# Layer 0's first eight units on the unscaled input, its first two half by half, and the input's hi halves one pair later

## The chip, the cores and the metric

The kernel runs on one core of a Trainium2 chip. The metric is device time in microseconds, from one launch to its end; three runs of the kernel before gave a median of 1510.79 us. "hi" and "lo" below are the two parts into which every fp32 operand is split, so that a product can be made of three fp32r matmuls (hi·hi, lo·hi, hi·lo).

## What is computed

One step of a two-layer decoder on 320 tokens (256 of a prompt, 8 x 8 of samples), width 1024, weights in fp32. Each layer, cut to what matters here:

```python
h = rms_norm(x, g_mix_pre)
proj = h @ w_in                      # split into q, k, v, g_ret, ca, cb, ga, gb
u = ca * sigmoid(cb)                 # conv branch: 16 units of weights, done first
z = conv(concat([c0, u]), conv_w)    # 31 taps per channel, depthwise
y_ret = (silu(g_ret) * layer_norm(retention(q, k, v, r0))) @ w_ret_out
x = x + rms_norm((sigmoid(ga)*y_ret + sigmoid(gb)*(silu(ln(z)) @ w_conv_out)) @ w_o, g_mix_post)
h2 = rms_norm(x, g_ffn_pre)
x = x + rms_norm((silu(h2 @ w_ffn_gate) * (h2 @ w_ffn_up)) @ w_ffn_down, g_ffn_post)
```

`rms_norm(x, g)` is x times g per channel times one factor per token. The factor (`rstd`) can be applied to x before the product with the weights, or to the product afterwards.

## The kernel before

All tensors lie with channels on partitions: x is 8 tiles of 128 channels by 320 tokens. The weights come as 360 units of 128 x 8 x 128 (512 KB), 180 per layer, in the order in which they are used, through a ring of four buffers. For each unit SyncE loads `wring`, ScalarE copies the hi part into `whi`, VectorE subtracts it and writes `wlo` (the helper `lower`), and TensorE runs 24 matmuls into one of four banks (`unit`). `split(l, u)` on ScalarE and on VectorE stands for unit u + 3 (AHEAD): it is made three units ahead, into the buffer that unit u - 1 gave back. Semaphores carry the order; within an engine the order is that of the code.

Units 0 to 15 of a layer are its input to the conv branch, in pairs: unit 2n gives cb, unit 2n + 1 gives ca of tile n. VectorE makes u of tile n (`up` for the prompt, `us` for the samples). Then come four heads of 12 units (`head`), and the rest.

Layer 0: ScalarE squares x, VectorE adds the squares, TensorE takes their mean, ScalarE makes `rstd`, and VectorE makes h (`normalised`): the value in `acc`, its hi part on ScalarE (`hhi`), its lo part (`hlo`). Only then does TensorE begin: `first_units` runs units 0 to 2 side by side, tile of h by tile of h; unit 3 and three rounds of four units (`cin_round`) follow, all on h.

Layer 1: units 0 to 7 (pairs n < FREE_PAIRS = 4) run on x times g only (`uhi`, `ulo`), while the statistics are taken in between; VectorE multiplies each product by `rstd` when it reads the bank (into `sig`, then `tmp`; both count `cin_step`). h for the rest is made along with these pairs, H_TILES = (0,1,2), (3,4,5), (6,7) tiles behind pairs 0, 1 and 2, and TensorE waits for all eight (`h_ready`) before unit 8:

```python
if free and n < len(H_TILES):
    for k in H_TILES[n]:
        h_value_of(l, k)
    if n:
        for k in H_TILES[n - 1]:
            h_low_of(l, k)
```

GpSimd works in layer 0 in this order: it starts the transfers (params, conv state, constants, two retention states), waits until all eight tiles of h are there (`h_ready`), computes the 30 old taps of the samples' convolution (`past_taps`, 60 tensor operations), stores the conv results (`cp_out`, `cs_out`), waits until these are stored, and then serves the heads: as soon as VectorE has updated a quad of retention states it stores the quad (`rs_out`) and loads the next but one (`state`) into the same buffer. TensorE reads that one in the next head's units (`late_query`, at unit 4, tile 3 and unit 5, tile 3).

Of the kernel before, what the change touches and what calls it, by code (L numbers as in the profile page):

```python
# [113 lines left out]
def program(nc, w, xin, consts, params, r_in, c_in, x_out, rp_out, rs_out, cp_out, cs_out):  # L114
    ctx = ExitStack()
    with ctx:
# [30 lines left out]
        gpre = sb("gpre", KT)  # L147
# [27 lines left out]
        past0 = sb("past0", KT, DB, DS, offset=go_at + (HEADS - 1) * 4 * T * 4 + KT * DB * DS * 4)  # L175
# [61 lines left out]
        gpre_loaded = sem("gpre_loaded")  # L237
# [23 lines left out]
        x_loaded, par_loaded, con_loaded = sem("x_loaded"), sem("par_loaded"), sem("con_loaded")  # L261
# [42 lines left out]
        def _(pool):  # L304
# [91 lines left out]

            pool.dma_start(par[:, :], params[0]).then_inc(par_loaded, 16)
# [4 lines left out]
            pool.dma_start(gpre[:, :], params[1, :, G_MIXPRE:G_MIXPRE + KT]).then_inc(gpre_loaded, 16)  # L402
            for l in range(DEPTH):
                for q in range(2):
                    load(l, q)
                if l == 0:
# [4 lines left out]
                    past_taps(0, past0, stap, par[:, G_CB:G_CW], par[:, G_CW:NPAR])  # L411
# [36 lines left out]
            pool.wait_ge(gpre_loaded, 16)  # L448
# [5 lines left out]
        def _(pe):  # L454
# [25 lines left out]
            def first_units(l, q, rhs, hi_ready, ready, between=None):  # L480

                pe.wait_ge(lo_done, l * UNITS + (q * RING + AHEAD))
                for k in range(UB):
# [10 lines left out]
                    if between is not None:  # L494
                        between(k)

# [218 lines left out]
            for l in range(DEPTH):  # L715

                if l == 0:
                    keep_clock(18)
                    for k in (0, 1, 4, 5):
                        pe.wait_ge(x_halves, k // 4 + 1)  # L720
                        mm = pe.matmul(X[:, 0:T], ones_d[:, :], sq8[:, k, :], start=(k == 0), stop=(k == 5))
                    mm.then_inc(stat_done, 1)
                    keep_clock(12)

                def x_half(i):

                    pe.wait_ge(x_halves, l * 2 + (i + 1))
                    if i == 0:
# [12 lines left out]
                def cin_round(i, rhs):  # L741
                    for j in range(4):
                        if j % 2 == 0:
# [5 lines left out]
                if l == 0:  # L749
                    first_units(l, 0, h_tile, lambda k: pe.wait_ge(h_hi, l * 16 + (k + 1)), lambda k: h_read(l, k))  # L750
                    unit(l, 0, AHEAD, AHEAD, h_tile)
                    with pe.Fori(1, 4) as i:
                        cin_round(i, h_tile)
                else:
                    first_units(l, 0, u_tile, lambda k: pe.wait_ge(ux_hi, (l - 1) * KT + (k + 1)), lambda k: pe.wait_ge(ux_ready, (l - 1) * KT + (k + 1)), between=x_both)
                    unit(l, 0, AHEAD, AHEAD, u_tile)
                    cin_round(1, u_tile)
                    pe.wait_ge(h_ready, l * 16 + KT)
                    with pe.Fori(2, 4) as i:
                        cin_round(i, h_tile)  # L760
# [108 lines left out]
        def _(act):  # L869
# [142 lines left out]
            log_exp_table()  # L1012
            act.wait_ge(x_loaded, 16)
            for k in range(KT):
                act.activation(sq8[:, k, :], x[:, k, :], ACT.Square).then_inc(sq_done, 1)
            act.wait_ge(memset_done, 2)
# [14 lines left out]
            for s in range(AHEAD - 1):  # L1031
                first_split(s)
            for l in range(DEPTH):
                if l:
                    split(l, U_CIN)
                act.wait_ge(stat_done, l * STATS + 1)
                rsqrt(l, X[:, 0:T], 0, 0)
                if l == 0:
                    first_split(AHEAD - 1)
                if l == 0:  # L1040
                    halves_of_h(l, range(KT))
# [686 lines left out]
```

## Time and profile before

| | |
|---|---|
| median of three runs | 1510.79 us (1508.86 to 1515.58) |
| time of the profiled execution | 1509.68 us |
| its span from first to last instruction | 1507.9 us, so 1.8 us lie around it |
| TensorE busy, share of the span | 97% |
| mean granted TensorE clock | 0.996 of 2.4 GHz |
| TensorE's first unit begins | 15.10 us |
| unit 8 of layer 0 begins | 43.37 us |
| unit 8 of layer 1 begins | 793.38 us |

The profile is of one execution. Each timeline row gives start, duration, engine, line and operation, and in brackets how long the engine sat idle before it and whose signal ended that. A matmul of a unit starts every 0.147 us at full clock, so a unit takes 3.52 us.

### The profile page before, as it was taken

The numbers are of one execution on the slowest core, as the hardware profiler recorded it, in microseconds if no ns is written. First come the engines' busy times: TensorE is split into PE (matmuls) and PEld (weight loads), VectorE is DVE, ScalarE is ACT, GpSimd is POOL, SyncE is SP. The second block draws the span as 40 slices with busy tenths as digits, with TensorE's granted clock in tenths as the row PEclk, the third lists the DMA queues.
The fourth block names the chain that finished last, engine by engine and source line by source line (L and its number), as shares of the span: only waits on it lengthen the run. The fifth ranks groups of instructions, "written<-read, shape, count | busy, mean of one in ns | idle before, by whom it ended". The sixth has DMA issues, their size and how long they took to land.

```text
span 1507.9 us, 25284 instructions
## 1 busy us (share of the span) xinstructions
PE 1466.7 (97%) x9684; PEld 1374.0 (91%) x9684; DVE 1138.6 (76%) x1771; ACT 678.8 (45%) x996; POOL 276.9 (18%) x254
## 2 busy tenths in 40 slices
PE   9999999999999999999989999999999999999997
PEld 8997978888999899999979979788799999999996
DVE  6999999989666677885478897989885766666544
ACT  5343534446454443443353445345554645434432
POOL 4991212120300002555100001122111000000000
PEclk9999999999999999999999999999999999999999
DMA  8447665855545254445535565757654442544453
GB/s 330 144 154 263 235 243 197 316 196 193 162 133 190 84 171 150 153 141 168 168 129 168 187 222 215 276 199 293 219 182 145 142 152 85 168 153 151 154 155 122
DMA packets 64970, 275.46 MB, mean 183 GB/s; under 512 B 7280, under 2 KB 7536, under 8 KB 55664
## 3 DMA queue, kind: packets, MB, share of 16 engines
q1 hardware_dynamic: 53280, 193.49, 39.2%
q0 software_dynamic: 11600, 80.74, 14.1%
q8 instruction: 61, 1.00, 0.3%
q14 instruction: 29, 0.24, 0.0%
HBM read 230.30 MB, written 43.89 MB: 182 GB/s over the span
## 4 chain that ended last, share of the span: by engine, by line
PE 78%; DVE 12%; DMA 4%; ACT 3%; issue 2%; POOL 0%; DVEq 0%; ACTq 0%; POOLq 0%
PE bank L466 23%; PE bank L468 22%; PE bank L467 22%; DVE wlo L1164 3%; DMA state<-r_in 3%; DVE acc L1207 2%; DVE state L1238 2%; DMA rs_out<-state 1%; PE bank L628 1%; PE bank L609 1%; PE bank L645 1%; PE bank L491 1%; DVE x L1560 1%; ACT whi L878 1%; PE bank L577 1%
## 5 line engine op out<-in xcount | busy, mean ns | idle before, releaser
L466 PE MATMUL bank<-hhi,whi 128*128 128x320 f32 x1976 | 638.3, 323 | 7.3 <-DVE hlo L1164 5.3
L1164 DVE TENSOR_TENSOR wlo<-wring,whi 128x1024 fp32r<-128x1024 f32 x363 | 483.8, 1336 | 186.7 <-ACT whi L878 159.7
L468 PE MATMUL bank<-hhi,wlo 128*128 128x320 f32 x1976 | 612.2, 310 | 0.0
L467 PE MATMUL bank<-hlo,whi 128*128 128x320 f32 x1976 | 612.0, 310 | 0.0
L466 PEld LDWEIGHTS bank<-hhi,whi 128*128 128x128 f32 x1976 | 372.3, 188 | 28.7 <-issue 27.6
L467 PEld LDWEIGHTS bank<-hlo,whi 128*128 128x128 f32 x1976 | 372.5, 189 | 8.8 <-issue 7.6
L468 PEld LDWEIGHTS bank<-hhi,wlo 128*128 128x128 f32 x1976 | 372.0, 188 | 0.0
L878 ACT ACTIVATE whi<-wring 128x1024 fp32r<-128x1024 f32 x264 | 277.2, 1054 | 206.2 <-PE bank L468 205.4
L1207 DVE SCALAR_TENSOR_TENSOR acc<-up,par,acc 128x256 f32<-128x256 f32 x480 | 210.5, 506 | 0.3
L904 ACT ACTIVATE whi<-wring 128x1024 fp32r<-128x1024 f32 x96 | 101.2, 1054 | 61.3 <-PE bank L468 58.1
L466 PE MATMUL bank<-fhi,whi 128*128 128x320 f32 x352 | 110.8, 315 | 0.0
L467 PE MATMUL bank<-flo,whi 128*128 128x320 f32 x352 | 108.8, 309 | 0.0
L468 PE MATMUL bank<-fhi,wlo 128*128 128x320 f32 x352 | 108.8, 309 | 0.0
L1238 DVE SCALAR_TENSOR_TENSOR state<-state,con,bank 128x512 f32<-128x512 f32 x128 | 88.9, 742 | 13.8 <-PE bank L645 13.7
L466 PE MATMUL bank<-ghi,whi 128*128 128x320 f32 x256 | 79.6, 311 | 2.5 <-DVE glo L1164 2.5
L468 PE MATMUL bank<-ghi,wlo 128*128 128x320 f32 x256 | 79.0, 309 | 0.0
L467 PE MATMUL bank<-glo,whi 128*128 128x320 f32 x256 | 79.0, 308 | 0.0
L1139 ACT ACTIVATE sig<-sig 128x320 f32<-128x320 f32 x44 | 20.8, 472 | 124.0 <-DVE sig L1594 124.0
L352 POOL DMA_DIRECT2D rs_out<-state x32 | 17.5, 546 | 317.4 <-DVE state L1238 317.4
L447 POOL DMA_DIRECT2D par<-params x2 | 1.2, 576 | 365.9 <-DVE acc L1548 365.9
L467 PEld LDWEIGHTS bank<-flo,whi 128*128 128x128 f32 x352 | 66.1, 188 | 0.6
L466 PEld LDWEIGHTS bank<-fhi,whi 128*128 128x128 f32 x352 | 66.1, 188 | 0.6
(193 smaller groups left out, 1923.2 us busy)
## 6 DMA issues: line engine op xcount, KB each, us to landing
wring<-w SPq DMA_DIRECT2D x364, 512.0 KB, 3.6
state<-r_in POOLq DMA_DIRECT2D x32, 1024.0 KB, 8.1
rs_out<-state POOLq DMA_DIRECT2D x32, 1024.0 KB, 5.0
rp_out<-pst POOLq DMA_DIRECT2D x8, 512.0 KB, 9.1
us<-c_in POOLq DMA_DIRECT2D x2, 1216.0 KB, 5.5
cs_out<-us POOLq DMA_DIRECT2D x2, 1216.0 KB, 8.8
cp_out<-up POOLq DMA_DIRECT2D x2, 1144.0 KB, 5.0
con<-consts POOLq DMA_DIRECT2D x1, 1421.0 KB, 9.7
```

The source lines that it names most:

```text
L352: pool.dma_start(rs_out[H * QUADS + q], state[q % 2][:, :, :]).then_inc(r_stored[q % 2], 16)
L466: pe.matmul(bank[g][:, 0:T], whi[j][:, k, :], hi, start=start and k == 0, stop=False)
L467: pe.matmul(bank[g][:, 0:T], whi[j][:, k, :], lo, start=False, stop=False)
L468: mm = pe.matmul(bank[g][:, 0:T], wlo[j][:, k, :], hi, start=False, stop=stop and k == n - 1)
L491: mm = pe.matmul(bank[j][:, 0:T], whi[j][:, k, :], lo, start=False, stop=(k == UB - 1))
L577: pe.matmul(b[0:n, o:o + m], qkv[:, 2 + d, j0:j0 + n], qkv[:, d, i0:i0 + m], start=(d == 0), stop=(d == 1))
L878: act.activation(whi[s][:, :, :], wring[s][:, :, :], ACT.Copy).then_inc(hi_done, 1)
L904: act.activation(whi[s][:, :, :], wring[s][:, :, :], ACT.Copy).then_inc(hi_done, 1)
L1139: act.activation(sig[:, n % 4, :], sig[:, n % 4, :], ACT.Silu).then_inc(sig_done, 1)
L1164: return dve.tensor_tensor(dst, value, hi.bitcast(F32), ALU.subtract)
L1207: dve.scalar_tensor_tensor(out=out, in0=src, scalar=tap, in1=out, op0=ALU.mult, op1=ALU.add).then_inc(conv_step, 1)
L1238: dve.scalar_tensor_tensor(out=st, in0=st, scalar=con[:, ds(hd + C_CD, 1)], in1=ring(pos)[:, :], op0=ALU.mult, op1=ALU.add).then_inc(dve_a ...
```

## The change

Layer 0 is treated as layer 1 was: units 0 to 7 on x times g, products scaled afterwards, h made along the way. Its first two units run in halves (`opening_half`: unit 0 tiles 0 to 3, unit 1 tiles 0 to 3, unit 0 tiles 4 to 7, unit 1 tiles 4 to 7), unit 2 whole with the statistics between its tiles. x is loaded in two halves, between the first weights. Params for layer 0's g come by a small transfer of their own. In both layers ScalarE makes the hi parts of a group of h tiles one pair later, behind the next unit's `whi`, and TensorE takes a bank again as soon as `cin_step` says that it was read. In rounds 1 and 2 it waits for `cin_step` in both layers; round 3 as before. The intermediate of the old taps moves to other buffers (`past`, `ptap`), since `ulo` now uses the old place; GpSimd's order is the same, its wait for `h_ready` too. The loops over rounds (`Fori`) are written out.

```diff
 SyncE
-            sp.dma_start(x[:, :, :], xin).then_inc(x_loaded, 16)
             for s in range(RING):
                 sp.dma_start(wring[s][:, :, :], w[s]).then_inc(w_ready[s], 16)
+                if s < 2:
+                    sp.dma_start(x[:, 4 * s:4 * s + 4, :], xin[:, 4 * s:4 * s + 4, :]).then_inc(x_loaded[s], 16)
 GpSimd
+            pool.dma_start(gpre[:, 0, :], params[0, :, G_MIXPRE:G_MIXPRE + KT]).then_inc(gpre_loaded[0], 16)
             pool.dma_start(par[:, :], params[0]).then_inc(par_loaded, 16)
...
                     pool.wait_ge(h_ready, KT)
-                    past_taps(0, past0, stap, par[:, G_CB:G_CW], par[:, G_CW:NPAR])
+                    past_taps(0, past, ptap, par[:, G_CB:G_CW], par[:, G_CW:NPAR])
 TensorE
+            def opening_half(j, k0):
+                pe.wait_ge(lo_done, j + 1)
+                for k in range(k0, k0 + UB // 2):
+                    pe.wait_ge(ux_hi, k + 1)
+                    pe.matmul(bank[j][:, 0:T], whi[j][:, k, :], uhi[:, k, :], start=(k == 0), stop=False)
+                    pe.matmul(bank[j][:, 0:T], wlo[j][:, k, :], uhi[:, k, :], start=False, stop=False)
+                    pe.wait_ge(ux_ready, k + 1)
+                    mm = pe.matmul(bank[j][:, 0:T], whi[j][:, k, :], ulo[:, k, :], start=False, stop=(k == UB - 1))
...
                 if l == 0:
-                    first_units(l, 0, h_tile, lambda k: pe.wait_ge(h_hi, l * 16 + (k + 1)), lambda k: h_read(l, k))
-                    unit(l, 0, AHEAD, AHEAD, h_tile)
-                    with pe.Fori(1, 4) as i:
-                        cin_round(i, h_tile)
+                    keep_clock(13)
+                    for j, k0 in ((0, 0), (1, 0), (0, 4), (1, 4)):
+                        opening_half(j, k0)
+                    unit(l, 0, 2, 2, u_tile, between=x_both)
...
+                unit(l, 0, AHEAD, AHEAD, u_tile)
+                cin_round(1, u_tile, scaled=False)
+                pe.wait_ge(h_ready, l * 16 + KT)
+                cin_round(2, h_tile, scaled=False)
+                cin_round(3, h_tile)
 ScalarE
                 for n in range(KT):
-                    if l == 0 or n:
+                    if n:
                         split(l, U_CIN + 2 * n)
-                    if l and n < FREE_PAIRS:
-                        act.wait_ge(cin_step, (l - 1) * (2 * FREE_PAIRS) + (2 * n + 1))
+                    if 0 < n <= len(H_TILES):
+                        halves_of_h(l, H_TILES[n - 1])
+                    if n < FREE_PAIRS:
+                        act.wait_ge(cin_step, l * (2 * FREE_PAIRS) + (2 * n + 1))
                         sigmoid(sig[:, n % 4, :], sig[:, n % 4, :])
...
                     split(l, U_CIN + 2 * n + 1)
-                    if l and n < len(H_TILES):
-                        halves_of_h(l, H_TILES[n])
 VectorE
-                    free = l > 0 and n < FREE_PAIRS
+                    free = n < FREE_PAIRS
```

What stands in a row on VectorE in the opening of layer 0, before (the numbers at buffers are the program's: `wring_49`, `whi_53`, `wlo_57` are buffer 0 of each, the next numbers buffers 1, 2, 3):

```order
L1402 TENSOR_TENSOR sq_84<-sq_84 128x640 x2
L1164 TENSOR_TENSOR wlo_57<-wring_49,whi_53 128x1024
L1164 TENSOR_TENSOR wlo_58<-wring_50,whi_54 128x1024
L1178 SCALAR_TENSOR_TENSOR acc<-x,par,rstd 128x320
L1164 TENSOR_TENSOR wlo_59<-wring_51,whi_55 128x1024
```

After them come the other seven values of h, each followed by a lo part. In the changed kernel the same place reads:

```order
L1177 TENSOR_TENSOR wlo_57<-wring_49,whi_53 128x1024
L1201 SCALAR_TENSOR_TENSOR ulo<-x,gpre,uhi 128x320 x4
L1177 TENSOR_TENSOR wlo_58<-wring_50,whi_54 128x1024
L1201 SCALAR_TENSOR_TENSOR ulo<-x,gpre,uhi 128x320 x4
L1177 TENSOR_TENSOR wlo_59<-wring_51,whi_55 128x1024
L1410 TENSOR_TENSOR sq_84<-sq_84 128x640 x2
L1429 MEMSET up 128x8x30
L1177 TENSOR_TENSOR wlo_60<-wring_52,whi_56 128x1024
L1442 TENSOR_TENSOR sig<-bank,rstd 128x320
L1177 TENSOR_TENSOR wlo_57<-wring_49,whi_53 128x1024
L1447 TENSOR_TENSOR tmp<-bank,rstd 128x320
```

The squares have moved behind three units' splits, the lo parts of x stand between them, and everything that needs `rstd` comes after unit 3's `wlo`.

On the same engine, from pair 2 to pair 3 of layer 0, the changed kernel has these rows (before, there were only the two `wlo`, `up`, `us` and the taps in `acc`):

```order
L1442 TENSOR_TENSOR sig<-bank,rstd 128x320
L1177 TENSOR_TENSOR wlo_57<-wring_49,whi_53 128x1024
L1447 TENSOR_TENSOR tmp<-bank,rstd 128x320
L1451 TENSOR_TENSOR up<-tmp,sig 128x256
L1452 TENSOR_TENSOR us<-tmp,sig 128x8x8
L1191 SCALAR_TENSOR_TENSOR acc<-x,par,rstd 128x320 x2
L1177 TENSOR_TENSOR hlo<-acc,hhi 128x320 x3
L1211 TENSOR_SCALAR acc<-up,par 128x256 x2
L1177 TENSOR_TENSOR wlo_58<-wring_50,whi_54 128x1024
L1177 TENSOR_TENSOR hlo<-acc,hhi 128x320 x2
```

The last row is the eighth tile of h, for which TensorE's unit 8 and GpSimd's first tap wait; it stood ahead of unit 3's `wlo` before, and now stands behind that of unit 9.

On ScalarE, layer 1's pairs 0 and 1 in the kernel before:

```order
L908 ACTIVATE sig<-sig 128x320
L878 ACTIVATE whi_53<-wring_49 128x1024
L1010 ACTIVATE hhi<-acc 128x320 x3
L878 ACTIVATE whi_54<-wring_50 128x1024
L908 ACTIVATE sig<-sig 128x320
```

and in the changed kernel (in layer 0 and in layer 1 alike):

```order
L918 ACTIVATE sig<-sig 128x320
L888 ACTIVATE whi_53<-wring_49 128x1024
L888 ACTIVATE whi_54<-wring_50 128x1024
L1020 ACTIVATE hhi<-acc 128x320 x3
L918 ACTIVATE sig<-sig 128x320
```

The hi parts of three h tiles have moved behind the `whi` of the next unit, so this `whi` no longer waits for VectorE's values.

## Rows read from the trace of the kernel before

**Rows 1.** The page: busy time by engine.

```profile
PE 1466.7 (97%) x9684; PEld 1374.0 (91%) x9684; DVE 1138.6 (76%) x1771; ACT 678.8 (45%) x996; POOL 276.9 (18%) x254
```

**Rows 2.** Busy time by stretch, layer 0: busy (instructions), granted clock, DMA share, GB/s.

```profile
21.90:43.00 21.10, 21.10 (x146) 21.10 (x145) 17.05 (x17) 10.08 (x13) 20.23 (x12) 1.00 0.74 258
...
43.00:99.00 56.00, 53.92 (x365) 53.23 (x364) 55.43 (x50) 19.11 (x23) 53.34 (x35) 1.00 0.39 127
...
115.60:134.40 18.80, 18.80 (x125) 14.87 (x123) 16.83 (x34) 8.66 (x13) 1.13 (x3) 1.00 0.62 221
```

**Rows 3.** Timeline of the opening: start, duration, engine, operation, idle before, releaser.

```profile
6.52 2.98 ACT L1015 ACTIVATE sq<-x 128x320 f32<-128x320 f32 x8 [4.49 <-DMA x<-xin]
...
9.56 0.54 POOL L395 DMA_DIRECT2D us<-c_in  x1 [7.59 <-DMA wring<-w]
...
10.49 2.36 DVE L1164 TENSOR_TENSOR wlo<-wring,whi 128x1024 fp32r<-128x1024 f32 x2
...
15.10 0.42 PE L487 MATMUL bank<-hhi,whi 128*128 128x320 f32 x1 [0.65 <-DVE wlo L1164]
```

**Rows 4.** Busy time by stretch in the opening; the last number is GB/s.

```profile
6.00:7.00 1.00, 1.00 (x7) 1.00 (x6) 0.00 (x0) 0.48 (x2) 0.00 (x0) 1.00 1.03 422
```

**Rows 5.** The chain of work in the opening: start, duration, what.

```profile
10.42 1.36 PE bank L721 x4
```

**Rows 6.** Timeline of TensorE where units 4 and 8 of layer 0 begin.

```profile
29.29 0.31 PE L466 MATMUL bank<-hhi,whi 128*128 128x320 f32 x1
...
43.37 0.31 PE L466 MATMUL bank<-hhi,whi 128*128 128x320 f32 x1
```

**Rows 7.** Timeline of layer 1's input: the input splits, then the first pairs.

```profile
755.17 1.02 ACT L1155 ACTIVATE uhi<-x,gpre 128x320 fp32r<-128x320 f32 x2 [1.14 <-DVE x L1560]
...
759.63 1.47 DVE L1611 SCALAR_TENSOR_TENSOR ulo<-x,gpre,uhi 128x320 fp32r<-128x320 f32 x3
...
765.88 0.53 ACT L889 ACTIVATE lnv<-bank,eps 128x320 f32<-128x320 f32 x1 [3.45 <-PE bank L731]
...
771.05 0.39 PE L466 MATMUL bank<-uhi,whi 128*128 128x320 f32 x1 [0.37 <-DVE wlo L1164]
...
774.78 1.23 DVE L1164 TENSOR_TENSOR wlo<-wring,whi 128x1024 fp32r<-128x1024 f32 x1 [1.49 <-ACT whi L878]
...
783.00 1.23 DVE L1164 TENSOR_TENSOR wlo<-wring,whi 128x1024 fp32r<-128x1024 f32 x1 [0.28 <-ACT whi L878]
...
793.38 0.63 PE L466 MATMUL bank<-hhi,whi 128*128 128x320 f32 x1 [5.26 <-DVE hlo L1164]
```

**Rows 8.** Busy time by stretch behind the wait in layer 1.

```profile
793.40:799.00 5.60, 5.60 (x22) 5.60 (x23) 4.08 (x10) 2.36 (x3) 0.00 (x0) 0.52 0.51 179
```

**Rows 9.** Timeline of GpSimd: first tap, store behind the last, first state store.

```profile
21.90 1.06 POOL L324 TENSOR_TENSOR past<-us,par 128x512 f32<-128x512 f32 x1 [9.71 <-DVE hlo L1164]
...
116.19 0.53 POOL L416 DMA_DIRECT2D cs_out<-us  x1
...
134.41 0.53 POOL L352 DMA_DIRECT2D rs_out<-state  x1 [17.68 <-DVE state L1238]
```

**Rows 10.** DMA of the conv state store, landing time.

```profile
DMA to landing us min/median/max: 8.5/8.8/9.0
```

**Rows 11.** The chain of work in head 1.

```profile
134.41 4.35 DMA rs_out<-state
...
139.04 8.58 DMA state<-r_in
```

**Rows 12.** Groups on VectorE, 43 to 99 us, while GpSimd computes.

```profile
L1164 DVE TENSOR_TENSOR wlo<-wring,whi 128x1024 fp32r<-128x1024 f32 x14 | 30.2, 2194 | 0.0
...
L1207 DVE SCALAR_TENSOR_TENSOR acc<-up,par,acc 128x256 f32<-128x256 f32 x14 | 17.3, 1283 | 0.0
```

**Rows 13.** The same groups, 140 to 174 us, while it does not.

```profile
L1207 DVE SCALAR_TENSOR_TENSOR acc<-up,par,acc 128x256 f32<-128x256 f32 x33 | 13.6, 478 | 0.0
...
L1164 DVE TENSOR_TENSOR wlo<-wring,whi 128x1024 fp32r<-128x1024 f32 x7 | 8.5, 1215 | 0.0
```

More of the change, by code:

```diff
@@ L447, in _ @@
                 pool.dma_start(par[:, :], params[l + 1]).then_inc(par_loaded, 16)
-            pool.wait_ge(gpre_loaded, 16)
+            for l in range(DEPTH):
+                pool.wait_ge(gpre_loaded[l], 16)
             pool.wait_ge(par_loaded, (DEPTH + 1) * 16)
@@ L715, in _ @@
             for l in range(DEPTH):
[L717 to L723, printed above, removed]
                 def x_half(i):
                     pe.wait_ge(x_halves, l * 2 + (i + 1))
-                    if i == 0:
+                    if l and i == 0:
                         pe.wait_ge(stat_read, l * STATS)
@@ L739, in x_both, with cin_round @@
                         x_half(1).then_inc(stat_done, 1)
-                def cin_round(i, rhs):
+                def cin_round(i, rhs, scaled=True):
                     for j in range(4):
-                        if j % 2 == 0:
+                        if not scaled:
+                            pe.wait_ge(cin_step, l * (2 * FREE_PAIRS) + (4 * (i - 1) + j + 1))
+                        elif j % 2 == 0:
                             pe.wait_ge(sig_done, l * SIGS + i * 2 + (j // 2 - 1))
@@ L1183, in h_low_of, with ux_low @@
                 lower(hlo[:, k, :], acc[:, k, :], hhi[:, k, :]).then_inc(h_ready, 1)
-            def normalised(l):
-                dve.wait_ge(rstd_done, l * RSTDS + 1)
-                for k in range(KT + 1):
-                    if k < KT:
-                        h_value_of(l, k)
-                    if k == 0:
-                        first_split(AHEAD - 1)
-                    if k >= 1:
-                        h_low_of(l, k - 1)
+            def ux_low(l, k):
+                dve.wait_ge(ux_hi, l * KT + (k + 1))
+                dve.scalar_tensor_tensor(out=ulo[:, k, :], in0=x[:, k, :], scalar=gpre[:, l, k:k + 1], in1=uhi[:, k, :].bitcast(F32),
+                                         op0=ALU.mult, op1=ALU.subtract).then_inc(ux_ready, 1)
             def conv_tap(l, pair, k):
@@ L1409, in first_split @@
                 lower(wlo[s][:, :, :], wring[s][:, :, :], whi[s][:, :, :]).then_inc(lo_done, 1)
-            for s in range(AHEAD - 1):
-                first_split(s)
+            first_split(0)
+            for k in range(4):
+                ux_low(0, k)
+            first_split(1)
+            for k in range(4, KT):
+                ux_low(0, k)
+            first_split(2)
+            for i in range(2):
+                x_squares(0, i)
             for l in range(DEPTH):
                 dve.wait_ge(par_loaded, l * 16 + 16)
-                if l == 0:
-                    normalised(l)
                 dve.memset(up[:, :, 0:PAD], 0.0).then_inc(pad_zeroed, 1)
@@ L1607, in _ @@
                 post(1, RS_POST2, SQ_POST2, G_FFNPOST, U_DOWN, 3)
-                def ux_low(k):
-                    dve.wait_ge(ux_hi, l * KT + (k + 1))
-                    dve.scalar_tensor_tensor(out=ulo[:, k, :], in0=x[:, k, :], scalar=gpre[:, k:k + 1], in1=uhi[:, k, :].bitcast(F32),
-                                             op0=ALU.mult, op1=ALU.subtract).then_inc(ux_ready, 1)
                 for i, (k, n) in enumerate(MIX_GROUPS):
```

57 lines of the change are left out of this document (27 added, 30 removed).

## The prediction, written before the changed kernel ran

> **What bounds the kernel now.** I read the page first: TensorE is busy for 1466.7 us [rows 1], so nearly every microsecond by which its units start later or earlier reaches the end. The views by stretch then show where another engine is close behind it. From 43 to 99 us of layer 0 VectorE is busy 55.43 of 56 us and GpSimd 53.34; TensorE is there at 53.92, so it already waits 2.1 us. From 21.9 to 43 us VectorE still has 4 us free (17.05 of 21.10) [rows 2]. The timeline of the opening gives what stands ahead of the first unit at 15.10 us [rows 3]. The timeline of layer 1 matters most: its first eight units are already done in the way that layer 0 now gets, so it is the measured model for it [rows 7]. Last, GpSimd's timeline and the chain of head 1 show what hangs on the moment at which h is complete [rows 9, 11].
>
> **The opening.** x (1280 KB, first in the queue) is used from 6.52 us, and the second weight unit has landed by 9.56 [rows 3]; the transfers move 422 GB/s [rows 4]. Behind the reordering the first half of x has 1152 KB up to its end, so it comes at about 6.4; the second half ends after 2304 KB, 1.05 MB more than x did before, 2.5 us at that rate: about 9.2. ScalarE needs 0.46 us per `uhi` (two take 1.02) and VectorE the same per `ulo` (three take 1.47) [rows 7]; two `wlo` take 2.36 [rows 3]. In a row on VectorE: `ulo` 0 to 3 done at 9.2, unit 1's `wlo` (its `whi` follows four `uhi`, so 9.5) at 10.7, `ulo` 4 to 7 at 12.6, unit 2's `wlo` at 13.8. TensorE can do half of unit 0 from about 7.2, waits for unit 1's `wlo` until 10.9, runs 36 matmuls of 0.147 us to 16.2, then unit 2 (3.5 us) with eight statistics matmuls between (four took 1.36 [rows 5]; I take 2.3 for all, since they overlap). The statistics end at 22.0. ScalarE's squares (2.98 us [rows 3]) start at 12.4, so they are in time. From the end of the statistics to unit 4 layer 1 took 5.17 us (765.88 to 771.05 [rows 7]), through two activations, a table load, the sigmoid, `whi`, `wlo`. So unit 4 begins at 27.2, against 29.29 [rows 6]: **-2.1 us**. The small transfer of g is the unknown: hidden, if it lands by 6.4; params took until before VectorE needed them and give no landing time of so small a piece. If it comes as late as the second weight unit did (9.56), all moves by 3.1 us, and that is the bound above; below it the gain cannot grow, since x sets the time.
>
> **Unit 8 and the tiles of h.** In layer 1 unit 8 began 22.33 us behind unit 4 (771.05 to 793.38), of which TensorE waited 5.26 us for the last lo part of h at once [rows 7]. The change takes away two waits of VectorE in this chain: its `wlo` waited 1.49 and 0.28 us for a `whi` that stood behind three `hhi` [rows 7]; with ScalarE's new order that `whi` is made before. **Layer 1: -1.8 us** (bounds 0, if the time comes back in the sigmoid's wait, and -2.7). The wait of 5.3 us stays, because TensorE's earlier units move up by as much.
> Layer 0 now gets the same chain: 22.3 - 1.8 = 20.5 us behind unit 4, so unit 8 at 47.7 against 43.37 [rows 6], where TensorE did not wait at all: **+4.3**. Behind such a wait the granted clock in layer 1 was 0.52, the 1.2 GHz level, for 5.6 us; 22 matmuls began where 38 would have [rows 8]. That is another **+2.7**. Layer 0's TensorE is then 7.0 us late.
>
> **GpSimd.** Its first tap waits for the same last tile of h. It began at 21.90 us; now it begins at 47.7, 25.8 us later. From the first tap to the issue of `cs_out` it needs 94.3 us (21.90 to 116.19 [rows 9]). Before, this was free: GpSimd then sat idle 17.68 us until the first retention state was ready at 134.41 [rows 9]. But ahead of serving the heads it also waits until `cs_out` has landed, 8.8 us by the median [rows 10]; so only some 9.5 us of the 17.68 were slack. I take 92.3 us for the taps instead of 94.3, as units in heads take TensorE a little longer, and fewer splits of VectorE fall into the stretch. Then: `cs_out` issued at 140.0, landed at 148.8, first state stored (4.35) and the next loaded (8.58, and 0.28 between) [rows 11] at 162.1. TensorE reads it in head 1's unit 4, and did so at 147.6, the very moment when it had landed: the chain store, load, read has no slack. So TensorE goes on there **+14.5 us** late, whatever it was late before; the 7.0 are swallowed. Had they been the only loss, it would have waited some 7 us at this place, and a wait of such length costs the clock again, as in layer 1: **+2.5**. Queued behind GpSimd's wait are the second store, both loads, then `rp_out`; all are shifted alike.
>
> **VectorE beside it.** Where GpSimd computes, a `wlo` takes 2.194 us and a tap 1.283 [rows 12], where it is silent 1.215 and 0.478 [rows 13]. For 14 and 14 of them in 56 us this is 25 us, 0.44 us lost per us. 25.8 us of this overlap leave a stretch with 4 us free and come to one (115.6 to 142) in which VectorE was busy 16.83 of 18.80 us [rows 2]: about 11 us later. With TensorE's 7 this makes 16 to 18 us late at 140 us, about as late as the state. The two run beside each other, and VectorE catches up while TensorE waits for the state, so I add nothing; it is the upper bound's reason.
> The Trainium skill bears on this in "SBUF — State Buffer", section "Who interferes with whom": VectorE with two SBUF inputs and GpSimd take one pair of ports by an exclusive lock, and the loser is blocked for the whole instruction. By that rule alone each of some 24 splits in the stretch would wait for about half a GpSimd operation, and the sum would be close to mine. The rows agree with it: the same instruction is 0.98 us longer beside GpSimd. It speaks against moving the taps to where VectorE is full.
>
> **Sum.** Against the profiled execution's own 1509.68 us (1.1 below the median of 1510.79): layer 0 +14.5 + 2.5, layer 1 -1.8, other edits nothing (a sigmoid or bank wait by `cin_step` is hidden by the wait for h; loops written out change the fetch of instructions, and the heads, already written out, show no wait for it). That is +15.2: **1524.9 us**, 0.9% slower than the median. A measurement of this kernel can tell about 0.5%, 7.5 us.
>
> **Rivals.**
> *The state chain does not bind, and nothing can be measured (0.21).* GpSimd's operations come in long and short ones: its first took 1.06 us [rows 9], while 94.3 us over 60 operations make 1.57 on the mean. If it needs less than about 84 us for the taps, `cs_out` has landed by 141.4, when the first state would be updated on a TensorE that is 7 us late. Then what is left is +7.0 - 1.8, and up to 4 of VectorE: 1515 to 1519, most of it within 0.5%. Against it: VectorE is as full in the new stretch as in the old. This is the case that ends as no slower.
> *h comes in time (0.07 faster).* If VectorE, with GpSimd silent until unit 8, needs 16 us instead of 20.5 from unit 4 to the last lo part, no wait remains at unit 8 in either layer: -2.1 in layer 0, and 5.3 + 2.7 + 1.8 back in layer 1, 1498 to 1503, provided that GpSimd's chain does not bind as well. The point of decision is unit 8 at 43.4 us. Against it stands layer 1's 22.3 us, with GpSimd silent too.
> *VectorE becomes the bound on top (0.12).* If its 11 us and the state chain add up instead of overlapping, because taps and splits still stand ahead of the next states, TensorE loses 6 to 12 more: 1531 to 1537.
> *As forecast (0.60)*: 1518.5 to 1530.
>
> **Range and chances.** I cut 0.07 + about 0.04 below and 0.09 above: 1509 to 1533; the likeliest case alone 1518.5 to 1530. Slower by over 0.5% (above 1518.3): 0.60 + 0.12 - a little at its lower edge = 0.70; within: 0.23; faster: 0.07.
>
> **What would show it.** Right: unit 4 of layer 0 near 27 us and unit 8 near 47.7 behind a wait of 5 us for `hlo`, with a clock near 0.5 behind it; GpSimd's first tap near 47.7, `cs_out` near 140; the first `rs_out` released by a DMA and not by VectorE, near 149; a wait of `late_query` for `state` of 5 us or more near 162. In layer 1 unit 8 some 20.5 us behind unit 4, behind a wait that still is 5 us. Wrong: an `rs_out` released by VectorE near 141 (then the second or third case), or no wait at unit 8.

## The result, and the profile after

The changed kernel takes 1522.86 us (median of six runs, 1521.29 to 1524.63) where the kernel before, on the same chip, takes 1511.28. The ratio is 1.0083, with a 95% interval of 1.0073 to 1.0093: it is slower. The profiled execution took 1522.84 us, 13.2 more than that of before; its span is 1520.7 us. The forecast was 1524.9, in a range of 1509 to 1533.

The page, busy time by engine (against [rows 1]):

```profile
PE 1466.7 (96%) x9650; PEld 1371.7 (90%) x9650; DVE 1149.5 (76%) x1787; ACT 682.6 (45%) x1004; POOL 273.4 (18%) x255
```

TensorE is busy for as long as before and VectorE for 10.9 us more; GpSimd's work is the same in kind. So the time lies in waits and in the clock. Busy time by stretch of layer 0 (columns as in [rows 2]):

```profile
46.90:52.40 5.50, 5.50 (x29) 5.50 (x30) 3.98 (x5) 2.74 (x5) 5.22 (x4) 0.74 0.43 141
52.40:109.00 56.60, 53.43 (x351) 52.73 (x351) 56.60 (x50) 17.82 (x22) 53.94 (x35) 0.97 0.38 125
109.00:131.00 22.00, 19.37 (x137) 18.84 (x136) 20.31 (x18) 10.44 (x19) 20.82 (x16) 1.00 0.43 137
131.00:149.40 18.40, 15.77 (x89) 10.67 (x87) 16.69 (x29) 5.89 (x8) 6.27 (x10) 0.91 0.58 210
```

From 52.4 to 109 us VectorE is busy all the time, beside a GpSimd that is just as busy. In the last stretch it is TensorE that stands still for part of the time (busy 15.77 of 18.40) and its granted clock has come down to 0.91 on the mean.

TensorE's timeline, where units 4 and 8 of layer 0 begin (against [rows 6]) and where it waits afterwards:

```profile
26.71 0.39 PE L469 MATMUL bank<-uhi,whi 128*128 128x320 f32 x1 [1.24 <-DVE wlo L1177]
...
46.81 0.63 PE L469 MATMUL bank<-hhi,whi 128*128 128x320 f32 x1 [4.97 <-DVE hlo L1177]
...
89.77 0.39 PE L469 MATMUL bank<-hhi,whi 128*128 128x320 f32 x1 [2.32 <-DVE wlo L1177]
...
126.39 1.22 PE L569 MATMUL bank<-con,qkv 128*128 128x128 f32 x8 [2.63 <-DVE kdec L1326]
...
138.14 1.71 PE L624 MATMUL bank<-vtok,stm 128*128 128x512 f32 x2 [2.63 <-DVE vst L1338]
...
162.76 1.05 PE L643 MATMUL bank<-state,qz 128*16 128x512 f32 x8 [0.65 <-DMA state<-r_in]
```

Unit 4 is 2.6 us earlier than before and unit 8 3.4 us later. The two waits of 2.63 us in the heads are new: before, TensorE waited for VectorE 2.1 us between 45 and 150 us, and never for `kdec` or `vst`. The read of the state at 162.76 is 15.1 us late, without a long wait of its own.

GpSimd's timeline (against [rows 9]):

```profile
46.94 1.06 POOL L325 TENSOR_TENSOR past<-us,par 128x512 f32<-128x512 f32 x1 [35.93 <-DVE hlo L1177]
...
137.29 0.53 POOL L418 DMA_DIRECT2D cs_out<-us  x1
...
149.44 0.53 POOL L353 DMA_DIRECT2D rs_out<-state  x1 [11.62 <-DVE state L1246]
...
155.78 0.53 POOL L307 DMA_DIRECT2D state<-r_in  x1 [2.52 <-DMA rs_out<-state]
```

The conv results were stored 21.1 us later than before and took 7.9 us to land, so until about 145.2. But the first `rs_out` came at 149.44 and was released by VectorE. The chain of work shows what VectorE was held up by:

```profile
128.63 3.48 DVE acc L1215 x4
...
133.34 1.47 DVE wlo L1177
134.81 2.61 DVE acc L1215 x4
137.42 0.67 DVE vst L1338
138.09 0.04 issue
138.14 1.71 PE bank L624 x2
```

Taps (`acc`) and splits (`wlo`) stand ahead of `vst`, for which TensorE waits; only behind that do the products and updates of the states come. Beside GpSimd they are slow; the groups on VectorE from 46.9 to 131 us (against [rows 12, 13]):

```profile
L1177 DVE TENSOR_TENSOR wlo<-wring,whi 128x1024 fp32r<-128x1024 f32 x20 | 41.2, 2100 | 3.2 <-ACT whi L914 1.7 <-ACT whi L888 1.5
L1215 DVE SCALAR_TENSOR_TENSOR acc<-up,par,acc 128x256 f32<-128x256 f32 x23 | 26.7, 1216 | 0.0
```

Layer 1's timeline (against [rows 7]):

```profile
782.71 0.53 ACT L899 ACTIVATE lnv<-bank,eps 128x320 f32<-128x320 f32 x1 [3.45 <-PE bank L738]
...
787.88 0.39 PE L469 MATMUL bank<-uhi,whi 128*128 128x320 f32 x1 [0.36 <-DVE wlo L1177]
...
807.98 0.63 PE L469 MATMUL bank<-hhi,whi 128*128 128x320 f32 x1 [4.97 <-DVE hlo L1177]
```

ScalarE takes its sigmoid when unit 8 has ended; these rows are first in layer 0, then in layer 1. Before:

```profile
47.15 0.44 ACT L908 ACTIVATE sig<-bank 128x320 f32<-128x320 f32 x1 [2.46 <-PE bank L468]
...
799.67 0.44 ACT L908 ACTIVATE sig<-bank 128x320 f32<-128x320 f32 x1 [3.83 <-PE bank L468]
```

In the changed kernel:

```profile
52.03 0.44 ACT L918 ACTIVATE sig<-bank 128x320 f32<-128x320 f32 x1 [2.47 <-PE bank L471]
...
813.20 0.44 ACT L918 ACTIVATE sig<-bank 128x320 f32<-128x320 f32 x1 [2.47 <-PE bank L471]
```

Layer 1 starts 16.8 us late (782.71 against 765.88); its unit 8 comes 20.1 us behind unit 4 instead of 22.3, and unit 8's sigmoid, 5.2 us later at 813.20, is 13.5 us late. So layer 0 costs 16.8 us and layer 1's input gives back 3.3.

### The profile page after: what moved, and what is told of

It reads as the page before. It is cut to its first block, busy times and chain, and to the rows that moved or that the text cites. A ratio compares the mean times of both kernels' runs of the same rounds, so it can differ in the third digit from the quotient of the medians.

```text
span 1520.7 us, 25221 instructions
## 1 busy us (share of the span) xinstructions
PE 1466.7 (96%) x9650; PEld 1371.7 (90%) x9650; DVE 1149.5 (76%) x1787; ACT 682.6 (45%) x1004; POOL 273.4 (18%) x255
## 4 chain that ended last, share of the span: by engine, by line
PE 76%; DVE 14%; DMA 3%; ACT 3%; issue 3%; POOL 0%; DVEq 0%; ACTq 0%; POOLq 0%
PE bank L469 22%; PE bank L471 22%; PE bank L470 22%; DVE wlo L1177 3%; DVE acc L1215 3%; DMA state<-r_in 2%; DVE state L1246 2%; PE bank L643 1%; PE bank L682 1%; ACT whi L888 1%; PE bank L660 1%; PE bank L624 1%; DVE x L1571 1%; DMA rs_out<-state 1%; DVE tmp L1569 1%
## 5 line engine op out<-in xcount | busy, mean ns | idle before, releaser
L469 PE MATMUL bank<-hhi,whi 128*128 128x320 f32 x1936 | 626.9, 324 | 13.1 <-DVE hlo L1177 9.9
L471 PE MATMUL bank<-hhi,wlo 128*128 128x320 f32 x1936 | 599.8, 310 | 0.0
L470 PE MATMUL bank<-hlo,whi 128*128 128x320 f32 x1936 | 599.8, 310 | 0.0
L469 PEld LDWEIGHTS bank<-hhi,whi 128*128 128x128 f32 x1936 | 365.4, 189 | 35.1 <-issue 23.5
L470 PEld LDWEIGHTS bank<-hlo,whi 128*128 128x128 f32 x1936 | 365.9, 189 | 9.1 <-issue 7.9
L471 PEld LDWEIGHTS bank<-hhi,wlo 128*128 128x128 f32 x1936 | 365.2, 189 | 0.0
L1215 DVE SCALAR_TENSOR_TENSOR acc<-up,par,acc 128x256 f32<-128x256 f32 x480 | 216.1, 520 | 0.5 <-issue 0.2
L328 POOL TENSOR_TENSOR past<-past,ptap 128x512 f32<-128x512 f32 (+7 forms) x58 | 86.7, 1495 | 4.5
```

Of the source, the lines that this page charges most:

```text
L328: pool.tensor_tensor(window(past, 0, n), window(past, 0, n), window(ptap, 0, n), ALU.add).then_inc(sample_conv_step, 1)
L469: pe.matmul(bank[g][:, 0:T], whi[j][:, k, :], hi, start=start and k == 0, stop=False)
L470: pe.matmul(bank[g][:, 0:T], whi[j][:, k, :], lo, start=False, stop=False)
L471: mm = pe.matmul(bank[g][:, 0:T], wlo[j][:, k, :], hi, start=False, stop=stop and k == n - 1)
L1215: dve.scalar_tensor_tensor(out=out, in0=src, scalar=tap, in1=out, op0=ALU.mult, op1=ALU.add).then_inc(conv_step, 1)
```

## The experiments

The theory after this reading: GpSimd's lateness costs some 10 us of the 15, by two paths. One is the state path of the prediction (conv results landed, quad stored, next loaded). The other is VectorE, whose slow stretch moves into the heads. The rival: VectorE's additional work and the wait for h cost it all.

| kernel | median us | ratio to before, 95% interval |
|---|---|---|
| changed kernel | 1522.9 | 1.0083 (1.0073 to 1.0093) |
| old kernel, late taps | 1520.5 | 1.0064 (1.0047 to 1.0081) |
| changed, early taps | 1532.3 | 1.0157 (1.0129 to 1.0184) |
| old kernel, layer 1's part alone | 1509.2 | 0.9991 (0.9982 to 1.0001) |
| changed, `whi` before the sigmoid | 1511.8 | 1.0017 (1.0007 to 1.0027) |
| the same, taps from unit 7 | 1512.8 | 1.0030 (1.0012 to 1.0048) |
| changed, no old taps | 1512.1 | 1.0009 (1.0000 to 1.0019) |
| no old taps, late store | 1522.4 | 1.0076 (1.0061 to 1.0092) |
| no old taps, late store, wait moved | 1520.9 | 1.0064 (1.0040 to 1.0087) |
| changed, store wait moved | 1522.1 | 1.0075 (1.0050 to 1.0100) |
| old, layer 1's part, `whi` first | 1501.6 | 0.9939 (0.9926 to 0.9953) |
| the same, x in halves | 1501.8 | 0.9940 (0.9921 to 0.9958) |

### GpSimd late, in the kernel before

```diff
-                    pool.wait_ge(h_ready, KT)
+                    pool.wait_ge(unit_done, 9)
```

> The kernel before with one edit: GpSimd begins its old taps when TensorE has finished nine units (about 46.9 us, the time of the changed kernel's first tap) and no longer when h is there (21.9 us). Nothing else is changed. Theory (most of the loss is GpSimd's lateness, by way of VectorE and the conv results' landing): VectorE is slowed later than before, in the heads, where it has less spare time; the conv results land near 145 us, VectorE releases the first quad of states near 142 to 145 us instead of 134.4, and the end comes 8 to 11 us later than before (about 1520). Rival (the loss lies in what layer 0's input itself adds, the wait for h and VectorE's additional work; lateness of GpSimd is harmless): 0 to +2 us (1511 to 1513).

Measured: 9.7 us slower (0.64% of 1509.6). GpSimd's timeline:

```profile
47.41 1.06 POOL L324 TENSOR_TENSOR past<-us,par 128x512 f32<-128x512 f32 x1 [35.03 <-PE bank L468]
...
136.59 0.53 POOL L416 DMA_DIRECT2D cs_out<-us  x1
...
145.17 0.53 POOL L352 DMA_DIRECT2D rs_out<-state  x1 [8.05 <-DMA cs_out<-us]
```

Here the first `rs_out` was released by the landing of the conv results, at 145.17. TensorE waited in the heads as in the changed kernel, for `kdec` and `vst`, and then for the state:

```profile
119.02 1.37 PE L554 MATMUL bank<-con,qkv 128*128 128x128 f32 x6 [3.06 <-DVE kdec L1318]
...
133.41 2.07 PE L609 MATMUL bank<-vtok,stm 128*128 128x512 f32 x2 [3.85 <-DVE vst L1330]
...
159.40 1.24 PE L628 MATMUL bank<-state,qz 128*16 128x512 f32 x8 [2.30 <-DMA state<-r_in]
```

Lateness alone thus costs 9.7 us, where the changed kernel is some 12.5 us slower than before by its ratio; the rival is out.

### GpSimd early, in the changed kernel

```diff
-                    pool.wait_ge(h_ready, KT)
+                    pool.wait_ge(unit_done, 3)
```

> The changed kernel with one edit: GpSimd begins its old taps when TensorE has finished three units (about 22 to 23 us, as early as in the kernel before) and no longer when h is there (46.9 us). Theory: VectorE's chain to h (the lo parts of the weights and of h between 23 and 42 us) then runs beside GpSimd, at about 1 us more for each of some eight wlo and 0.3 for each smaller operation; the wait ahead of unit 8 grows from 5.0 us to 14 to 17 us, while the later lateness goes; the two about cancel: 1518 to 1528. Rival (what costs is the lateness alone, h has slack enough): the wait ahead of unit 8 stays under 8 us and the time falls by about 10 us, to 1511 to 1514.

Measured: 1532.3, slower still. TensorE's timeline, and VectorE's groups from 27 to 67 us:

```profile
34.81 0.60 PE L469 MATMUL bank<-uhi,whi 128*128 128x320 f32 x1 [3.92 <-DVE wlo L1177]
...
50.17 0.61 PE L469 MATMUL bank<-uhi,whi 128*128 128x320 f32 x1 [5.39 <-DVE wlo L1177]
...
68.13 0.64 PE L469 MATMUL bank<-hhi,whi 128*128 128x320 f32 x1 [12.28 <-DVE hlo L1177]
```

```profile
L1177 DVE TENSOR_TENSOR hlo<-acc,hhi 128x320 fp32r<-128x320 f32 x8 | 11.2, 1452 | 0.0
L1191 DVE SCALAR_TENSOR_TENSOR acc<-x,par,rstd 128x320 f32<-128x320 f32 x8 | 8.7, 1132 | 0.0
```

The rival is out, and the theory's time was missed too, by over 4 us. The wait for h grew, if less than expected (12.28 us for 14 to 17), but three waits for `wlo`, 10.8 us together (1.8 in the changed kernel), stand ahead of it, and unit 8 begins 21.3 us later than in the changed kernel. A `hlo` took 1.452 us there instead of 0.490, a value of h 1.132 instead of 0.548; I had allowed 0.3 us more for each of these. Sixteen such operations stand ahead of unit 8.

### Layer 1's part alone

```diff
 TensorE, rounds 1 and 2 of layer 1
-                        if j % 2 == 0:
+                        if not scaled:
+                            pe.wait_ge(cin_step, (l - 1) * (2 * FREE_PAIRS) + (4 * (i - 1) + j + 1))
+                        elif j % 2 == 0:
...
 ScalarE, layer 1
+                    if l and 0 < n <= len(H_TILES):
+                        halves_of_h(l, H_TILES[n - 1])
...
                     split(l, U_CIN + 2 * n + 1)
-                    if l and n < len(H_TILES):
-                        halves_of_h(l, H_TILES[n])
```

> The kernel before with layer 1's part of the change alone (hi parts of h one pair later, banks taken when cin_step says that they were read); layer 0 is as before. The changed kernel's trace shows layer 1's input 3.3 us shorter than before (unit 8's wait 2.0 shorter, the clock back 1.2 earlier). Theory: that is independent of layer 0, so 3.3 us faster: 1507 to 1509. Rival (the gain in layer 1 came from VectorE's or the ring's state left by layer 0, not from this part): 0 to -1 us.

Measured: 1.4 us faster by the ratio (-2.7 to +0.2), so neither side is settled by the time. In the trace the stretch from layer 1's second `lnv` (766.99) to the sigmoid of unit 8 (798.49) takes 31.5 us, against 33.8 before and 30.5 in the changed kernel. So the edit gave 2.3. The further 1.0 in the changed kernel came with the clock: from the end of the same wait (4.98 us here, 4.97 there) to that sigmoid it took 6.24 us here and 5.22 there, with a granted clock of 0.58 and 0.71. That difference shows between executions of the same code as well (last section), so I count only the 2.3 as the edit's.

### `whi` before the sigmoid

```diff
                     if n < FREE_PAIRS:
+                        split(l, U_CIN + 2 * n + 1)
                         act.wait_ge(cin_step, l * (2 * FREE_PAIRS) + (2 * n + 1))
                         sigmoid(sig[:, n % 4, :], sig[:, n % 4, :])
...
-                    split(l, U_CIN + 2 * n + 1)
+                    if not (n < FREE_PAIRS):
+                        split(l, U_CIN + 2 * n + 1)
```

> The changed kernel with one edit in both layers: in the four free pairs ScalarE copies whi of the pair's second unit before it waits for VectorE's scaled product and takes the sigmoid, not after. In the trace of the changed kernel VectorE waits 1.2 to 1.5 us ahead of the second wlo of each of these pairs for that whi. Theory (those waits are a serial part of the chain that ends at h): the wait ahead of unit 8 shrinks from 5.0 us by 4 to 5 us in both layers and the clock isn't lowered there, together 5 to 7 us per layer, of which layer 0's is kept only in so far as GpSimd starts earlier too: 1508 to 1514. Rival (VectorE is busy throughout and the waits are slack that it would spend anyway later in the pair): unit 8's wait stays over 3.5 us, 1521 to 1523.

Measured: 1511.8, by the ratios 10 us faster than the changed kernel. Its rows, TensorE first in layer 0, then in layer 1:

```profile
42.08 0.42 PE L469 MATMUL bank<-hhi,whi 128*128 128x320 f32 x1 [2.55 <-DVE hlo L1179]
...
798.12 0.55 PE L469 MATMUL bank<-hhi,whi 128*128 128x320 f32 x1 [1.85 <-DVE hlo L1179]
```

The wait fell from 4.97 to 2.55 and 1.85 us, less than the 4 to 5 us expected, since the units ahead of it came earlier too: unit 8 begins 4.7 us earlier. Layer 1's stretch from `lnv` to the sigmoid takes 26.2 us instead of 30.5. In the changed kernel VectorE had waited for these `whi` 2.24, 1.49 and 1.49 us ahead of unit 8 of layer 0; the last of them:

```profile
39.82 1.23 DVE L1177 TENSOR_TENSOR wlo<-wring,whi 128x1024 fp32r<-128x1024 f32 x1 [1.49 <-ACT whi L888]
```

Of these 5.2 us 0.46 are left here. The 4.8 us that are gone are the 4.7 by which unit 8 begins earlier: the waits were serial.

Then GpSimd's taps in that kernel six microseconds earlier:

```diff
-                    pool.wait_ge(h_ready, KT)
+                    pool.wait_ge(unit_done, 7)
```

> The changed kernel with whi ahead of the sigmoid in both layers, and GpSimd's old taps begun when TensorE has finished seven units (about 36 us) instead of with h (42.2 us in the run with that order alone, 1511.8 us). Theory (each us of GpSimd's lateness costs 0.4 us at the end: 25 us later cost 10.9): 6 us earlier gives 2.5 back, and the last lo parts of h beside GpSimd cost 1 to 2 us ahead of unit 8: 1509 to 1512. Rival (no price on the h chain this late): 1507 to 1509.

Measured: 1512.8, no gain, and above the range of either. TensorE paid on the chain to h:

```profile
50.78 0.64 PE L469 MATMUL bank<-hhi,whi 128*128 128x320 f32 x1 [11.37 <-DVE hlo L1179]
```

Unit 8 comes 8.7 us later for a start 6.1 us earlier. The end can't be told from that without this edit: the intervals overlap, and layer 1's `lnv` comes at 777.60 here and at 777.39 there. So nearly all that is lost ahead of unit 8 is saved in the heads, where TensorE no longer waits for `kdec` and `vst` (2.83 and 3.13 us without this edit).

### The two paths apart

First the old taps shrunk to next to nothing, one channel tile and one sample each, so that part of the convolution is left out. This stands around each operand of the multiplication and the addition:

```diff
+                def small(a):
+                    return a[:, 0:1, 0:1] if l == 0 and k else a
```

> The changed kernel with GpSimd's old taps of layer 0 cut to one channel tile and one sample each, after the first (58 of 60 operations; part of the convolution is left out), so that GpSimd is done by about 60 us and hardly works beside VectorE. The wait for h ahead of unit 8 stays. Theory (of the 15 us by which layer 0 ends later, 4.9 are the wait for h with its clock and the rest is GpSimd's lateness, by VectorE and the state transfers): 1506 to 1512, and no wait of TensorE for kdec and vst. Rival (VectorE's additional work alone makes TensorE wait in the heads): the waits of 2.6 us for kdec and vst stay, 1517 to 1523.

Then the same (the same part is left out), with the conv results held back:

```diff
+                if l == 0:
+                    pool.wait_ge(unit_done, 30)
                 pool.dma_start(cp_out[l], up[:, :, :])
```

> As the run without old taps (the same part of the convolution is left out), but GpSimd holds the conv results back until TensorE has finished 30 units, about 136 us, as late as the changed kernel stores them. So VectorE is fast and only the state transfers are late. Theory A (the states are a second path nearly as long as VectorE's): conv results landed near 145, first quad stored and next loaded by 158 to 159, where TensorE would be ready near 152: a wait of 5 to 7 us for the state with a lowered clock behind it, 6 to 10 us above the run without taps, 1513 to 1519. Theory B (VectorE's lag is the whole loss, the transfers have slack): no wait of TensorE for the state above 1 us, within 2 us of the run without taps.

Measured: 1512.1 without taps, some 11 us less than the changed kernel, and 1522.4 with the late store. Without taps, GpSimd and TensorE:

```profile
136.44 0.53 POOL L355 DMA_DIRECT2D rs_out<-state  x1 [57.89 <-DVE state L1248]
```

```profile
150.16 1.05 PE L645 MATMUL bank<-state,qz 128*16 128x512 f32 x8 [1.05 <-DMA state<-r_in]
```

With the late store:

```profile
136.81 0.53 POOL L422 DMA_DIRECT2D cs_out<-us  x1
146.29 1.06 POOL L355 DMA_DIRECT2D rs_out<-state  x2 [8.95 <-DMA cs_out<-us]
```

```profile
159.61 1.91 PE L647 MATMUL bank<-state,qz 128*16 128x512 f32 x8 [10.17 <-DMA state<-r_in]
```

The waits for `kdec` and `vst` are gone in both. With VectorE fast, the state path alone costs 10.3 us, and layer 1's `lnv` comes at 782.92, against 782.71 in the changed kernel. Theory A holds in kind; the wait is 10.2 us where 5 to 7 were expected, and the time above the 1513 to 1519 that I gave. That is just what the prediction described, a wait for the state with the clock lost behind it (0.82 granted from 159.6 to 170 us), only in a kernel whose VectorE isn't slowed.

Last, GpSimd's wait for the landing put behind the first head's states, once with the old taps in and once without:

```diff
-                pool.wait_ge(u_saved, l * 32 + 32)
                 for hd in range(HEADS - 1):
                     head(l, hd, False)
+                    if hd == 0:
+                        pool.wait_ge(u_saved, l * 32 + 32)
```

> The changed kernel with one edit: GpSimd waits for the landing of the conv results not before but after it has served the first head's states, so that the first quad is stored as soon as VectorE releases it. In the changed kernel the results landed near 145 us and VectorE released the quad at 149.4. Theory (VectorE's lag under the old taps is by itself as long as the state path): nothing to gain, 1521 to 1525, first rs_out within 1 us of 149.4. Rival (the late landing is what costs): first rs_out near 136 to 145 and 4 us or more faster, 1510 to 1518.

Measured: 1522.1, nothing gained; the first quad was released by VectorE again, 1.4 us earlier than in the changed kernel, where I had expected at most 1:

```profile
148.00 0.53 POOL L353 DMA_DIRECT2D rs_out<-state  x1 [10.07 <-DVE state L1247]
```

So in the changed kernel the late landing didn't decide; VectorE's lag alone is as long.

> The run without old taps and with the late store (1522.4 us; the same part of the convolution is left out), with GpSimd's wait for the landing of the conv results moved behind the first head's states. There TensorE waited 10.2 us for a state at 159.6 us. Theory (that wait hangs on the order of GpSimd's wait alone): the conv results are issued at 136.8, the first quad's store right behind them near 137.3, and the time falls by 7 to 10 us, to 1512 to 1515. Rival (the transfers are late because they share the queue and the memory with the conv results, whatever GpSimd waits for): the wait for the state stays over 5 us, 1517 to 1522.

Measured: 1520.9. The rival is right here. GpSimd and TensorE:

```profile
137.55 0.53 POOL L355 DMA_DIRECT2D rs_out<-state  x1
...
150.28 0.54 POOL L307 DMA_DIRECT2D state<-r_in  x1 [9.47 <-DMA rs_out<-state]
```

```profile
156.69 1.91 PE L648 MATMUL bank<-state,qz 128*16 128x512 f32 x8 [7.03 <-DMA state<-r_in]
```

The store left 8.7 us earlier, but it went out right behind 2.3 MB of conv results and took 12.4 us to land, where the first such store takes 4.2 to 6.5 in the other traces. Some two thirds of the wait (7.03 of 10.17 us) stay without GpSimd's order, beside transfers that crowd at this place. Whether they crowd in the queue or in the memory, no run shows.

### The faster kernel

Layer 1's part from above and, in the free pairs of layer 1 alone, `whi` before the sigmoid:

```diff
                     if l and n < FREE_PAIRS:
+                        split(l, U_CIN + 2 * n + 1)
                         act.wait_ge(cin_step, (l - 1) * (2 * FREE_PAIRS) + (2 * n + 1))
...
-                    split(l, U_CIN + 2 * n + 1)
+                    if not (l and n < FREE_PAIRS):
+                        split(l, U_CIN + 2 * n + 1)
```

> The kernel before in layer 0; in layer 1 the change's part (hi parts of h one pair later, banks taken on cin_step) and, in the four free pairs, whi of the pair's second unit copied ahead of the sigmoid. In the run with that order in both layers, the stretch of layer 1 from its second lnv to the sigmoid of unit 8 took 26.2 us, against 33.8 in the kernel before and 31.5 with layer 1's part alone. Theory (this stretch does not depend on layer 0): 7.6 us faster than before, 1501 to 1504. Rival (the time that layer 1's input gives back is lost again in the first head, where VectorE then runs later against TensorE): at most 3 us faster, 1506 to 1509.

Measured: 1501.6 us, 9.2 less than before (0.61%, interval 0.47 to 0.74%). From `lnv` at 766.83 to the sigmoid of unit 8 at 791.43 it needs 24.6 us, 9.2 fewer than before, and nothing is lost again in the heads. Unit 8 of layer 1:

```profile
787.55 0.41 PE L466 MATMUL bank<-hhi,whi 128*128 128x320 f32 x1 [1.84 <-DVE hlo L1168]
```

The granted clock was 1.00 over the whole stretch. The 1.6 us beyond the 7.6 expected are the clock: from that wait's end to the sigmoid it took 3.88 us, and 5.42 behind the wait of 1.85 us in the kernel with the order in both layers. That doesn't hang on layer 0's form: the run with the taps from unit 7, whose layer 1 is the same code as in that kernel, took 3.88 us too.

Then x in two transfers:

```diff
-            sp.dma_start(x[:, :, :], xin).then_inc(x_loaded, 16)
+            for s in range(2):
+                sp.dma_start(x[:, 4 * s:4 * s + 4, :], xin[:, 4 * s:4 * s + 4, :]).then_inc(x_loaded[s], 16)
...
-            act.wait_ge(x_loaded, 16)
             for k in range(KT):
+                if k % 4 == 0:
+                    act.wait_ge(x_loaded[k // 4], 16)
```

> The fastest kernel so far (layer 1's part with whi ahead of the sigmoid, 1501.6 us, layer 0 as before) with x loaded in two transfers, so that ScalarE squares the first four tiles before the rest is there. In the kernel before the squares begin at 6.52 us, when the whole x has landed, and take 2.98 us. Theory (the statistics' chain sets the opening): first half landed about 1.2 us earlier, the last square ends 1.0 to 1.4 us earlier, 1500.2 to 1500.7. Rival (the second half lands as late as the whole x did, and its four squares then bound, or the weights land later by the second transfer): 0 to 1 us faster or no change, 1500.8 to 1502.5.

Measured: 1501.8, no difference that can be told. The trace has most of what was expected of the opening:

```profile
5.11 1.55 ACT L1020 ACTIVATE sq<-x 128x320 f32<-128x320 f32 x4 [3.07 <-DMA x<-xin]
7.10 1.55 ACT L1020 ACTIVATE sq<-x 128x320 f32<-128x320 f32 x4 [0.44 <-DMA x<-xin]
```

The squares end at 8.65 instead of 9.50 us (1.0 to 1.4 earlier was expected), and TensorE's first unit begins at 14.23 instead of 15.12 us. The 0.9 us are there, and below what the runs resolve.

## Why the prediction was right, and where it was not

- *Opening, -2.1*: right; unit 4 at 26.71 for 27.2, -2.6. g's small transfer was the one that released ScalarE's first `uhi`, at 6.54 us, not at the 9.56 of the bound.
- *Unit 8, +4.3*: right in kind; at 46.81 for 47.7, behind a wait of 4.97 us for `hlo`. It is +3.4: unit 4 was 0.5 us earlier than forecast, and the stretch from there to unit 8 took 20.1 us, not 20.5.
- *The clock behind it, +2.7*: mis-sized for this trace. From the end of the wait to the first sigmoid it took 5.22 us in both layers of the changed kernel, 6.29 in layer 1 before, 3.78 undisturbed (43.37 to 47.15 us, layer 0 before): the cost is 1.4 us here and was 2.5 there. I took one instance for the price. Four of the runs have the changed kernel's code up to there in layer 0, and behind the same wait of 4.96 to 4.98 us they lost 1.6, 2.0, 2.0 and 2.9 us.
- *GpSimd*: right in kind, 3.6 us too long. First tap 25.0 us later (25.8), 90.4 us for the taps (92.3), landed at 145.2 (148.8).
- *"The state chain", +14.5 and +2.5 of clock*: this step failed as an account of the changed kernel, though not in its sum. The state was free of GpSimd about 4 us before VectorE released it; no wait of 5 us or more stood at `late_query`, only 0.65, and `rs_out` was released by VectorE, at 149.44. The time of that place was nevertheless met (15.1 us late), because the other path was at least as long. That was luck: with the landing at 145.2 and the 13.3 us that store and load took here, the state path by itself would have been some 11 us late (an estimate from this trace), and in the run with VectorE relieved it appeared as predicted, 12 us late, behind 10.17 us of wait.
- *The +2.5 of clock behind that place* did not come: the granted clock was 1.00 from 162.8 to 200 us. Until layer 1 the lateness grew by 1.7 us all the same, in later heads, where TensorE waited 2.6 us for states between 231 and 362 us (0.3 before). Layer 0 as a whole came out at 16.8 us for the 17.0 forecast, from other parts than forecast.
- *VectorE "beside it", "I add nothing"*: the lag of 16 to 18 us was sized about right (`rs_out` 15.0 us late), and its role was wrong. TensorE doesn't run on while VectorE lags: it needs `kdec` and `vst` from it, and waited for both before it came to the state. From unit 8's sigmoid, 4.9 us late, the delay grew to 15.0 us at 149.4: 6.2 by more waiting for VectorE (8.3 us instead of 2.1), the rest mostly by the clock (0.97 and 0.91 of the stretches above). That the two paths don't add was right, as the run without taps and the one with the late store bracket it.
- The sign named for an error, an `rs_out` released by VectorE, did appear, at 149 and not near 141. The first rival, in which the state chain doesn't bind, had that right and the time wrong (1515 to 1519), as it allowed VectorE 4 us; the third had VectorE bind, but on top of the state chain (1531 to 1537).
- *Layer 1, -1.8*: -3.3 in the trace of the changed kernel, and 2.3 in the run with that part alone. From unit 4 to unit 8 it was 2.2 us, so the two waits were read rightly; the rest is clock. What I overlooked are the waits of 1.49 us beside them, one in each pair, that the new order leaves: the runs with `whi` before the sigmoid took them away as well, and 6.9 of the 9.2 us of the faster kernel came with that (the stretch fell from 31.5 to 24.6 us, 2.4 of it behind the wait for h, where the clock stayed full).
- *Interference*: the rule of the Trainium skill ("SBUF — State Buffer", "Who interferes with whom") agrees with the changed kernel's rows: a split beside GpSimd 2.100 us, 0.88 longer than alone, a tap 1.216, 0.74 longer; half of a GpSimd operation is 0.75 us there (90.4 us for 60). Starting the taps earlier showed that it also bears on the small operations, `hlo` 1.452 us.

What would have done better: with two late paths that meet at one instruction, name the one with the larger lag as the bound and say that the other comes within a few microseconds. I had both lags (14.5 and 16 to 18) and set the larger aside.

Not tried: the changed kernel with VectorE's taps moved out of head 1. How much of the 10 us is the clock alone stays open too.

## What to carry to other kernels

Speeding up the start of one engine moves whatever hangs on its last step; here a signal that was 3 us late for TensorE was 25 us late for GpSimd, whose slow neighbourhood then fell on the heads. Before optimising a transfer chain or an engine's lag, test each with the other removed: two paths of one length hide each other, and removing one gives nothing. And where a chain alternates between engines, look for the copy that stands behind a wait of its own engine: moving four of them per layer ahead of a sigmoid gave back 10 of the some 12.5 us that the change had cost, and together with layer 1's part of the change it made the kernel before 9.2 us faster.

## What the runs showed of the hardware

- Waits of one length cost different amounts of clock. Measured from the wait's end to unit 8's sigmoid, against 3.78 undisturbed: 4.97 us of wait lost 1.4 in both layers of the changed kernel, 4.98 lost 2.5 in layer 1 of the old kernel with the same order there; 1.84 us lost 0.1 in one kernel and 1.85 lost 1.6 in another. It differs between executions of the same code, too: up to this place in layer 0 the run with the store wait moved is the changed kernel, and it lost 2.9 us behind the same wait, 6.68 us at 0.54 against 5.22 at 0.71 (the number ahead of the last two is the granted clock). Runs don't show what makes the difference. The changed kernel, then that run:

```profile
46.81:52.03 5.22, 5.21 (x26) 5.22 (x27) 3.70 (x5) 2.37 (x3) 4.85 (x4) 0.71 0.39 123
```

```profile
46.72:53.40 6.68, 6.68 (x26) 6.68 (x27) 5.16 (x7) 2.37 (x4) 6.24 (x5) 0.54 0.50 157
```

- Beside GpSimd small operations of VectorE took two to three times as long: `hlo` 1.452 us against 0.49, a value of h 1.132 against 0.55 (both in the changed kernel, where GpSimd was silent).
- One 1 MB store issued right behind 2.3 MB of other stores took 12.4 us to land; the first such store took 4.2 to 6.5 us in the other traces.
